# Expert weights in one transfer for each piece, and the first projections of the second block in another order

## The reference, cut to what matters

```python
def first_block(x, ...):
    for i in range(DEPTH):                     # 2 layers
        z = rms_norm(h, g_mix[i]) @ w_in[i]    # then three mixers
        h = h + concat([y_a, y_b, y_c]) @ w_out[i]
        hn = rms_norm(h, g_ffn[i])
        f = swiglu(hn, ...) if i % 2 == 0 else moe_swiglu(hn, router_w, router_b, moe_w1, moe_w3, moe_w2)
        h = h + f                              # moe: silu(x @ w1) * (x @ w3) @ w2 of the chosen experts
        gate = jax.nn.sigmoid(rms_norm(h, g_ple[i]) @ ple_gate_w[i])
        h = h + (p[i] @ ple_proj_w[i]) * gate
    return rms_norm(h, g_final)

def second_block(x, c, ...):
    for l in range(DEPTH):                     # 2 layers
        sh1, sc1, g1, sh2, sc2, g2 = jnp.split(silu(c) @ ada_w[l] + ada_b[l], 6)
        h = rmsnorm(x, norm_mix_g[l]) * (1.0 + sc1) + sh1
        u = h @ w_in[l]                        # 1024 -> 2564 columns, then four mixers
        x = x + g1 * (mix @ w_out[l])
        h = rmsnorm(x, norm_ffn_g[l]) * (1.0 + sc2) + sh2
        x = x + g2 * ((silu(h @ ffn_w1[l]) * (h @ ffn_w3[l])) @ ffn_w2[l])
    return rmsnorm(x, final_g)
```

## Time and profile before

| | before |
|---|---|
| median of 3 runs | 2066.65 us (2066.28 to 2071.18) |
| profiled execution: time, span | 2066.58 us, 2065.3 us |
| granted TensorE clock, mean | 0.996 |
| busy: TensorE, VectorE, ScalarE | 97%, 47%, 20% |
| expert weights: transfers of 2 MB and 1 MB | 87 and 90 |
| expert stage, about | 643 to 1343 us of the span |

### The profile page before, as it was taken

How to read it: one execution, slowest core, us unless ns; L and a number is a source line. 1 busy time by engine, 2 the same in 40 slices (tenths; PEclk the granted TensorE clock), 3 DMA queues, 4 the chain that set the end, 5 groups by cost and what they waited for, 6 DMA issues and landing times.

```text
span 2065.3 us, 31417 instructions
## 1 busy us (share of the span) xinstructions
PE 2006.2 (97%) x13165; PEld 1192.4 (58%) x13165; DVE 969.3 (47%) x1732; ACT 412.5 (20%) x913; POOL 66.7 (3%) x69
## 2 busy tenths in 40 slices
PE   8999999999998999999999999999999999999998
PEld 5675997465754334323323233355689945669973
DVE  2564899736754000000000000147769984847676
ACT  2464000133452000000101001052420002331001
POOL 0021000000110000000000000100000000000000
PEclk9999999999999999999999999999999999999999
DMA  6223976355307999999999999837467742345430
GB/s 244 94 115 118 363 276 242 136 213 204 132 4 281 403 424 412 414 424 410 424 410 424 424 424 423 368 136 278 158 278 284 276 177 81 133 189 209 163 143 31
DMA packets 72852, 534.03 MB, mean 259 GB/s; under 512 B 12368, under 2 KB 12944, under 8 KB 30720
## 3 DMA queue, kind: packets, MB, share of 16 engines
q1 hardware_dynamic: 56032, 473.28, 57.0%
q10 hardware_dynamic: 14256, 51.91, 6.5%
q0 software_dynamic: 2416, 6.75, 0.9%
HBM read 527.28 MB, written 4.69 MB: 258 GB/s over the span
## 4 chain that ended last, share of the span: by engine, by line
PE 69%; DVE 20%; DMA 5%; ACT 3%; issue 2%; POOL 0%; DVEq 0%; ACTq 0%; SPq 0%
PE ps L92 69%; DVE ring L92 13%; DMA ring<-in_moe 4%; DVE transposed L92 3%; ACT ring L92 2%; DVE ada_chunks L92 1%; DVE z L92 1%; DVE natural L92 1%; DVE stat L92 1%; DMA ada_chunks<-in_c 0%; ACT natural L92 0%; POOL ring L92 0%; ACT z L92 0%; ACT L92 0%; DVE residual L92 0%
## 5 line engine op out<-in xcount | busy, mean ns | idle before, releaser
L92 PE MATMUL ps<-ring 128*32 128x512 f32 (+8 forms) x5968 | 871.3, 441 | 21.1 <-DMA ring<-in_moe 10.2
L92 PEld LDWEIGHTS ps<-ring 128*128 128x128 f32 (+4 forms) x5968 | 466.1, 151 | 361.1 <-issue 333.9
L92 PE MATMUL ps<-ring,transposed 128*128 128x384 f32 (+3 forms) x1344 | 462.8, 499 | 5.1 <-DVE transposed L92 4.5
L92 PEld LDWEIGHTS ps<-ring,transposed 128*128 128x128 f32 x1344 | 251.7, 191 | 187.6 <-issue 65.9
L92 PE MATMUL ps<-ring,z 128*32 128x512 f32 (+4 forms) x1718 | 326.7, 580 | 0.3 <-ACT z L92 0.3
L92 DVE TENSOR_TENSOR z<-z,ps 128x256 f32<-128x256 f32 (+4 forms) x80 | 34.6, 433 | 619.0 <-ACT z L92 598.2
L92 DVE TENSOR_TENSOR ring<-ring 128x512 f32<-128x512 f32 (+3 forms) x320 | 275.8, 862 | 17.3 <-ACT ring L92 0.8
L92 PEld LDWEIGHTS ps<-ring,z 128*32 128x32 f32 (+3 forms) x1718 | 110.2, 129 | 194.5 <-issue 191.7
L92 PE MATMUL ps<-natural,ring 128*128 128x128 f32 (+1 forms) x1472 | 174.6, 275 | 0.6 <-DVE natural L92 0.6
L92 PEld LDWEIGHTS ps<-natural,ring 128*128 128x128 f32 x1472 | 169.6, 192 | 1.2 <-DVE natural L92 1.0
L92 ACT COPY z<-ps 128x256 f32<-128x256 f32 (+6 forms) x112 | 46.9, 419 | 505.0 <-PE ps L92 493.1
(11 more groups left out here) (169 smaller groups left out, 1106.9 us busy)
## 6 DMA issues: line engine op xcount, KB each, us to landing
ring<-in_moe SPq DMA_DIRECT2D x87, 2048.0 KB, 21.0
ring<-in_moe SPq DMA_DIRECT2D x90, 1024.0 KB, 19.2
ring<-in_ffn_up SPq DMA_DIRECT2D x66, 1024.0 KB, 7.0
ring<-in_w_in SPq DMA_DIRECT2D x25, 1536.0 KB, 7.5
ring<-in_ffn_down SPq DMA_DIRECT2D x33, 1024.0 KB, 6.9
ring<-in_ada ACTq DMA_DIRECT2D x55, 512.0 KB, 6.3
ada_chunks<-in_ada ACTq DMA_DIRECT2D x38, 512.0 KB, 6.7
ring<-in_w_out SPq DMA_DIRECT2D x12, 1536.0 KB, 7.8
```

What stands on the lines that cost most here:

```text
L92: self.ins = None if self.book.counting else op(*args, **kw)
```

## The change

Each piece of the experts' weights is loaded by one transfer of 3 MB instead of one of 2 and one of 1 (piece 0 keeps three, of 1 MB each), and it is issued when both the up and the down products of piece n-5 are done. TensorE waits for the whole piece before its up products; the wait before the down products is then met already. Beside it, in the second block, projection (1, 0) moves ahead of the turn of token block 1, with PSUM banks renamed so that the first two tiles have a bank each, and VectorE modulates block 0 of mixb0 ahead of `dve_ple(1, 5)`.

```diff
+    def win_bank(s, t, i):
+
+        return t if s[:4] == "mixb" and t < 2 else i
@@ pe_win
-        b = (2 * t + i) % 2
+        b = win_bank(s, t, i)
...
-            if t:
+            if s[:4] == "mixb" and t < 3:
+                for freed in {(0, 1): ("z00",), (1, 1): ("z10",), (2, 0): ("z01",), (2, 1): ("z11",)}.get((t, i), ()):
+                    pe.wait_ge(f"{s}.{freed}")
+            elif t:
                 pe.wait_ge(f"{s}.z{t - 1}{i}")
@@ sp_moe
-        def load(n, part, at, freed, value):
+        def load(n):
...
             else:
-                sp.until(freed, value)
...
+                sp.until("moe_waves", PIECE_WAVES[n - RING_PIECES] + 1)
+                sp.until("moe_freed", n - RING_PIECES + 1)
             if n:
-                load(n - 1, "down", slice(4 * D, 6 * D), "moe_freed", n - RING_PIECES)
+                sp.load(piece(n), src, f"up{n % RING_PIECES}", f"moe.up{n}")
+                if book.counting:
+                    book.value[f"moe.down{n}"] = book.value[f"moe.up{n}"]
+                return
...
@@ pe_mixers2
         win(0, 0)
+        win(1, 0)
         pe_turn_h(s, 1)
         win(0, 1)
-        win(1, 0)
         win(1, 1)
@@ act_mixers2
-        act_modulate_xt(s, 1, gains[:, 0:8], mod[:, 0:8])
...
         load_ada(5)
         z(0, 0)
+        z(1, 0)
+        act_modulate_xt(s, 1, gains[:, 0:8], mod[:, 0:8])
         load_ada(2)
         z(0, 1)
-        load_ada(2)
-        z(1, 0)
-        load_ada(2)
+        load_ada(4)
         z(1, 1)
@@ dve_second
         dve_ple(1, 4)
+        dve_modulate_xt("mixb0", 0, gains[:, 0:8], mod[:, 0:8])
         dve_ple(1, 5)
-        dve_modulate_xt("mixb0", 0, gains[:, 0:8], mod[:, 0:8])
         dve_final("final1", 1, h, "mixb0.h")
```

More of the change, by code:

```diff
@@ L491, in act_z @@
             act.wait_ge(f"{s}.rstd{i}")
-            act(S.activation, z[:, i, t * COLS:t * COLS + n], ps[:, (2 * t + i) % 2, 0:n], ACT.Identity, scale=stat[:, i:i + 1])
+            act(S.activation, z[:, i, t * COLS:t * COLS + n], ps[:, win_bank(s, t, i), 0:n], ACT.Identity, scale=stat[:, i:i + 1])
         else:
-            act(S.copy, z[:, i, t * COLS:t * COLS + n], ps[:, (2 * t + i) % 2, 0:n])
+            act(S.copy, z[:, i, t * COLS:t * COLS + n], ps[:, win_bank(s, t, i), 0:n])
         act.then_inc(f"{s}.z{t}{i}")
@@ L2214, in load @@
                 order[x] = nc.values_load(order_i[0:1, x:x + 1], engines=(EngineType.SP,), min_val=0, max_val=NPIECE * (NE - 1))
+            src = d["moe"][p if book.counting else order[x] + p]
             if n < RING_PIECES:
@@ L2219, in load @@
             else:
-                sp.until(freed, value)
[L2221 to L2230, removed]
-            if n:
-                load(n - 1, "down", slice(4 * D, 6 * D), "moe_freed", n - RING_PIECES)
+                sp.until("moe_waves", PIECE_WAVES[n - RING_PIECES] + 1)
+                sp.until("moe_freed", n - RING_PIECES + 1)
+            if n:
+                sp.load(piece(n), src, f"up{n % RING_PIECES}", f"moe.up{n}")
+                if book.counting:
+                    book.value[f"moe.down{n}"] = book.value[f"moe.up{n}"]
+                return
+            ups = slice(0, 4 * D)
+            by_half = lambda ap: ap[:, ups].rearrange("p (h k n) -> p h k n", h=2, k=2)
+            sp.load(by_half(piece(n))[:, :, 0], by_half(src)[:, :, 0], "first", "moe.first")
+            sp.load(by_half(piece(n))[:, :, 1], by_half(src)[:, :, 1], "up0", "moe.up0")
+            sp.load(piece(n)[:, 4 * D:6 * D], src[:, 4 * D:6 * D], "down0", "moe.down0")
+        for n in range(len(PIECES)):
+            load(n)
     def dve_mo_select(x):
```

## The result

| | kernel before | changed kernel |
|---|---|---|
| median | 2067.19 us (4 runs) | 2190.24 us (2188.41 to 2195.27, 4 runs) |
| ratio | | 1.0593, 95% interval 1.058 to 1.0607 |
| profiled span | 2065.3 us | 2187.1 us, mean granted clock 0.973 |

The change costs 123 us; the forecast was 2143 (2108 to 2172). The direction and the mechanism were right, the size was 47 us short and outside the range.

The account below looks back on a forecast made before the run. TensorE, 97% busy, and the expert weights' DMA stream were taken as level, with the transfers' lead keeping TensorE fed. 2066.6 + 60 (waits) + 21 (clock) - 4.6 (projections) = 2143 us, range 2108 to 2172.

Parts of the forecast that it names:

- the mechanism: Expert stage: pieces issued later and awaited whole land after TensorE wants them, and its longer waits drop the clock.
- Sum 70.5 us ... +60 us: Expert stage: TensorE's waits for weights total 70.5 us, including today's 10.2, so +60 us.
- the walk: Expert waves stepped through all 88 pieces: landing 9.7 us after issue alone, 7.4 us when queued; waits sum to 70.5 us.
- In the stretch of the 128-token expert ... it costs next to nothing: Waves 0 to 18: over a whole wave lies between a freed place and its next use, so next to no cost.
- I take 21 us: Expert stage: half clock after long waits, 2.7 us per 7.3 us wait, 1.9 per 4.2; 21 us, bounds 0 and 29.
- at the border: Waves 22, 26, 46, 50: waits of about 3.2 us may or may not drop the clock, 0 to 1.9 us each.
- 0 to 15 us, and I take 0: POOL's gathers and stores in the expert stage delay awaited pieces by 0 to 15 us; priced at 0.
- -4.6 us: Projections: -2.6 us in mixb0 from VectorE's earlier modulation, -2.0 us from mixb1's covered gap; bounds -5 and +1.
- today's order had no gap there, so it gives nothing in mixb0: mixb0: projection (1, 0) moved ahead of the turn of block 1 fills no existing gap, so 0 us.
- the loads of projection 3 are issued 2.4 us later ... nothing: Projections: those loads have a lead of some 7 us, so no cost; 2 us if that cover is gone.
- rival 4: Everything above its estimate: gathers hit awaited pieces, small waits fall into the half clock too; 2172 us, chance 0.15.

Follow-up runs that it names:

- e3_early_whole: Kernel before, early issue and two transfers a piece kept, but TensorE waits for the whole piece before its up products: 2110.43 us, ratio 1.0209.
- e4_late_split: Issue as late as in the changed kernel, but two transfers of 2 and 1 MB with a signal each; ratio to the kernel before 1.0348, 2141.13 us.
- e1_merge: Only the experts' weights' part of the change, projections as in the kernel before: 2190.7 us, ratio 1.0606.
- e8_quiet: e1_merge with POOL's token gathers and stores cut to 8 columns of each row or half row, output not the reference's: 2178.71 us, ratio 1.0531.
- e5_filled: e1_merge with matmuls nobody reads put into its waits for weights, 16 or 7 ahead of fifteen waves: 2159.12 us, ratio 1.0436.
- e9_quiet_before: Kernel before with POOL's token gathers and stores cut to 8 columns of each row or half row, output not the reference's: 2053.45 us, ratio 0.9937.
- e7_mix_gate: Only the projections' part on the kernel before, with the conformer gate ahead of the last three ada sums on VectorE: 2066.9 us, ratio 0.9993.

## Why the prediction was wrong, point by point

Of the missing 47 us the profiled executions show 45.5: 2066.6 + 84.1 (waits) + 34.5 (clock) + 3.3 (projections) = 2188.5 us, against 2066.6 + 60 + 21 - 4.6 = 2143.

**"Sum 70.5 us ... +60 us": the mis-sized term, 24 us short.** The mechanism held to the wave. By wave:

| waves | forecast | measured |
|---|---|---|
| 23, 27, 39, 47, 51 | 36.5 | 39.8 |
| 19, 31, 43, 55 | 17 | 17.2 |
| 22, 26, 46, 50 | 13 | 17.5 |
| all others | 4 | 19.8 (5.14 at wave 4, 3.75 at 38, 2.54 at 35, 2.10 at 59 ...) |

Two things made the rest longer. A lone piece lands 10.0 to 11.2 us after its issue, 10.25 in the median of 14, not 9.7; the same walk with that gives 74.7 us in place of 70.5. And the walk let pieces land at even steps. In the trace of the changed kernel 67 of pieces 6 to 87 were issued over 1 us ahead of the landing of the one before; they landed 7.11 us after it at the least, 7.52 in the median and 11.19 at most, 32 of them more than 7.6 us after it. With these measured steps in place of the even ones the walk gives 93 us, where 94.3 were measured. The three streams that the experiments add have much the same surplus over the even walk (an estimate, as all walks are): e3_early_whole 41.3 us of waits against 17.0, e4_late_split 59.3 against 38.2, e1_merge 97.5 against 74.7, and the kernel before 10.2 against 0. So some 20 us of the changed kernel's waits, and 21 to 24 us in the three streams, come from uneven landings once the lead no longer covers them, whatever the issue and size.

About half of that is POOL's traffic. Eleven of the 67 queued pieces had packets of POOL's queue beside them, and they landed 9.7 us after the one before in the mean, the other 56 after 7.6; ten of the twelve steps over 8.5 us are among the eleven. With an even step for these eleven alone the walk falls from 93 to some 84 us. In e8_quiet, without the traffic, the pieces at these places take 7.7 us. But others take up to 10.1 there, so its waits fell by 5.1 us only. Between the first and the last signal of a piece's sixteen lie 1.8 us in the median. What delays a piece where POOL moves nothing I can't tell from the trace; it stays open.

**"In the stretch of the 128-token expert ... it costs next to nothing": wrong.** 5.14 us at wave 4 and 1.5 to 1.6 us each at 11 and 18. The lead there was above zero, but small: wave 4 waited for piece 6, which landed 10.7 us after piece 5 and not 7.3.

**"I take 21 us" (clock): 13.5 us short, and outside the bounds (29).** The price of one wait was right, 2.9 us behind the long ones against 2.7, and 1.7 behind a 4.15 us wait against 1.9. The count was wrong: the waits forecast at 3.2 us "at the border" were 4.1 to 4.8 and brought the half clock, up to 2.6 us each, and so did those at waves 4 and 38, and even the 2.10 us at wave 59. e5_filled shows the whole: 31.6 us back. The Trainium skill (TensorE: Matmul & The Clock Gate, Part 1: The HAM clock gate) has activity release the clock; e5_filled agrees, with 1.00 granted where its waits were filled.

**"0 to 15 us, and I take 0" (gathers and stores): right for the difference,** by e8 and e9. The traffic is not free in the changed kernel, but it costs the kernel before as much.

**The projections, "-4.6 us": wrong, +3.3.** The gaps of 1 us in mixb0 and the end of mixb1's 2.00 us came as written. The failed step is "today's order had no gap there, so it gives nothing in mixb0". It gave less than nothing: between the turn and the conformer gate that projection was work that covered VectorE's sums, and "the loads of projection 3 are issued 2.4 us later ... nothing" looked at who needs those loads, not at whose chunks they collide with on the DMA engines.

**The range.** Its top, rival 4, had named both overruns. It summed waits and clock with 15 us for gathers, which are not in the difference, and had no term for uneven landing.

## What to carry to other kernels

Where two streams are level, the queued lead is what pays for every irregularity. So price a change that shortens the lead with the unevenness of the landings (here 20 to 24 us over 88 pieces), not with their mean step, and then let each wait that grows past 3 or 4 us (one of 2.10 us did too) carry its slower matmuls too. When work is moved ahead of a turn, look at what it used to cover behind it, down to the order of the other engine's instructions; and read in the profile which engine sets the pace of the next 50 us before counting a gap as won. A signal for the part that is needed first is worth having even where the number of transfers is not.

## What the runs showed of the hardware

- The stretches of half clock inside the kernel lasted 3.41, 6.83 or 10.24 us. In the changed kernel there was one of 10.24 around each of the five waits of 7.8 to 8.3 us, which began during the wait; with seven of the ten waits of 3.4 to 5.2 us went one of 3.41. Waits of 2.37 us in the kernel before and of 2.54 us at wave 35 of the changed one had none, that of 2.10 us at wave 59 had one of 3.41, and in e7_mix_gate 10.24 us followed a wait of 1.46 us, so the length of the last wait alone does not decide it.
- Extra matmuls can save time: 7.2 us of them in an 8 us wait give back 2.9 us.
- 3.146 MB in one transfer land 10.0 to 11.2 us after the issue with the queue empty, 10.25 in the median, and 7.3 us after the one before in a queue that runs evenly; as transfers of 2 and 1 MB issued together, the second landed 10.0 us after the first issue (e4_late_split, 914.8 to 924.8 us).
- Small gathers and stores of POOL's queue delay the weights that land beside them: 9.7 us from one queued 3 MB piece to the next in place of 7.6, and 12 to 15 us of the kernel's time (e8_quiet, e9_quiet_before).
